# Two logarithms moved from ScalarE's table to a series on VectorE, in a two-block transformer kernel, with the four phases' issue orders rewritten

## The reference

```python
def rg_lru_group(xa, ya, conv_w, conv_b, ga_w, ga_b, gx_w, gx_b, lam):
    ...
    log_a = -LRU_C * r.astype(jnp.float32) * jax.nn.softplus(-lam.astype(jnp.float32))
    a = jnp.exp(log_a)
    ...

def forgetting_attention_group(q, k, v, f_logit, f_bias):
    ...
    log_f = jax.nn.log_sigmoid((f_logit + f_bias).astype(jnp.float32))
    ...
    c = jnp.cumsum(log_f, axis=1).transpose(0, 2, 1)
```

## Time and profile before

| | us |
|---|---|
| median of 3 runs | 962.14 (959.21 to 962.55) |
| the profiled execution | 962.55 |
| its span, first to last instruction | 960.8 |
| mixer, to the end of the output product | 0 to 212 |
| feed-forward, then the two layers | to 400, 680 and the end |

### The profile page before, as it was taken

The page is one execution under the profiler, slowest core; times in us unless marked ns, Lnnn a source line. Parts: engine busy times, 40 slices in busy tenths (PEclk is TensorE's granted clock), DMA queues, the critical chain, the costliest instruction groups (busy, mean ns, idle before and its releaser), DMA issues.

```text
span 960.8 us, 19359 instructions
## 1 busy us (share of the span) xinstructions
PE 923.4 (96%) x7806; PEld 852.2 (89%) x7806; DVE 702.0 (73%) x1061; ACT 522.7 (54%) x939; POOL 223.3 (23%) x194
## 2 busy tenths in 40 slices
PE   6899998889999999989999999999899999999997
PEld 6887996688999998879999899999699998999995
DVE  5887985558898897477877775576658787655684
ACT  7555264445665665374655574545555665555443
POOL 2324522232122121003314040033023322310140
PEclk9899998898999999999999999999999999999999
DMA  8433220043555556537545426555374444545551
GB/s 313 141 123 111 67 78 16 1 155 132 177 195 178 183 172 192 186 114 300 169 160 176 152 80 208 180 194 181 117 285 156 153 154 134 174 154 189 185 176 44
DMA packets 41560, 150.18 MB, mean 156 GB/s; under 512 B 4608, under 2 KB 4864, under 8 KB 41216
## 3 DMA queue, kind: packets, MB, share of 16 engines
q1 hardware_dynamic: 39456, 141.54, 43.9%
q10 hardware_dynamic: 2016, 7.41, 2.1%
HBM read 147.88 MB, written 1.05 MB: 155 GB/s over the span
## 4 chain that ended last, share of the span: by engine, by line
PE 92%; DVE 4%; ACT 2%; issue 1%; DMA 0%; DVEq 0%; SPq 0%; ACTq 0%
PE ps L724 90%; PE ps L1019 2%; DVE wlo L1637 1%; PE ps L1122 0%; DMA raw<-in_ws 0%; ACT whi L1233 0%; DVE S L1637 0%; DVE rw_pe L1862 0%; ACT L1233 0%; DVE ht L1645 0%; DVE rw_X L1637 0%; DVE pcraw L1637 0%; ACT tmp L1233 0%; DVE rr L1679 0%; DVE AR L1637 0%
## 5 line engine op out<-in xcount | busy, mean ns | idle before, releaser
L1233 ACT ACTIVATE whi<-raw 128x1024 fp32r<-128x1024 f32 (+1 forms) x264 | 278.2, 1055 | 314.9 <-PE ps L724 308.4
L724 PE MATMUL ps<-xh,whi 128*128 128x256 f32 (+2 forms) x1408 | 406.9, 289 | 20.5 <-DVE wlo L1637 8.2
L1637 DVE TENSOR_TENSOR wlo<-raw,whi 128x1024 fp32r<-128x1024 f32 (+1 forms) x256 | 324.4, 1271 | 114.6 <-ACT whi L1233 113.8
L724 PE MATMUL ps<-xl,whi 128*128 128x256 f32 (+2 forms) x1408 | 401.6, 285 | 1.4 <-DVE xl L1645 1.3
L724 PE MATMUL ps<-xh,wlo 128*128 128x256 f32 (+2 forms) x1408 | 400.8, 285 | 0.0
L724 PEld LDWEIGHTS ps<-xh,whi 128*128 128x128 f32 x1408 | 268.9, 191 | 26.5 <-issue 20.6
L724 PEld LDWEIGHTS ps<-xl,whi 128*128 128x128 f32 x1408 | 268.3, 191 | 2.6 <-DVE xl L1645 2.0
L724 PEld LDWEIGHTS ps<-xh,wlo 128*128 128x128 f32 x1408 | 269.2, 191 | 0.0
L724 PE MATMUL ps<-yh,whi 128*128 128x256 f32 x232 | 65.3, 281 | 0.0
L2213 POOL TENSOR_TENSOR gts<-gts 128x256 f32<-128x256 f32 x32 | 30.3, 955 | 150.5 <-DVE gts L1645 149.9
L724 PE MATMUL ps<-yl,whi 128*128 128x256 f32 x232 | 65.2, 281 | 0.0
(11 more groups left out here) (337 smaller groups left out, 1320.9 us busy)
## 6 DMA issues: line engine op xcount, KB each, us to landing
raw<-in_ws SPq DMA_DIRECT2D x262, 512.0 KB, 3.5
h<-in_rel ACTq DMA_DIRECT2D x2, 1024.0 KB, 13.2
qc<-in_gam ACTq DMA_DIRECT2D x3, 512.0 KB, 5.1
mt<-in_m ACTq DMA_DIRECT2D x2, 576.0 KB, 5.9
h<-in_hT SPq DMA_DIRECT2D x4, 272.0 KB, 5.4
gts<-in_lng ACTq DMA_DIRECT2D x2, 512.0 KB, 7.6
out<-ht SPq DMA_DIRECT2D x4, 256.0 KB, 2.0
gts<-in_g ACTq DMA_DIRECT2D x2, 448.0 KB, 10.0
```

Source lines behind the costliest of these rows:

```text
L724: return e.matmul(o, l, r, start=start, stop=stop, skip_group_check=True)
L1233: return e.activation(o, a, f, bias=bias, scale=scale, accum_out=acc)
L1637: return e.tensor_tensor(o, a, b, op)
```

## The change

Three edits are made.

1. ACT's Ln goes, in `la_a` and in `fo_log`. ACT still takes Abs and Exp.
2. DVE computes log(1 + u) as 2 atanh(u / (u + 2)) in a new helper `log1p`, 13 operations in three parts of 4, 5 and 4, each operation waiting for the one before. It is run once on 128x2 (steps `la.a`, `la.b 0`, `la.b 1`) and once on 8x272 (steps `fo.log 0` to `fo.log 2`). The factor 2 is taken up by `fo.sum` and `la.c`.
3. The strings of `WEAVE` for the mixer and for both layers are new; those of the feed-forward are as before. The steps are the same but for those of edit 2.

```diff
-        "f": [("fo.proj",), ("fo.log",), ("fo.sum",), ("fo.lr",)],
+        "f": [("fo.proj",)] + [("fo.log", n) for n in range(3)] + [("fo.sum",), ("fo.lr",)],
...
-        "n": [("la.a",), ("la.c",)],
+        "n": [("la.a",), ("la.b", 0), ("la.b", 1), ("la.c",)],
...
         "dve": (
-            "dmwddwddwddwddsndwwwwddfdmmmdfdmwwdsdmwdwmmdwmdwdwwddrrrwrwrfwwrreeeoeeorsrrrworwdsswssrddrrrddloo"
+            "dmwnnnndddddwwwdsdddwdwwdddwfmmdmmfsddwwrrrwdddrrrdfwrdwwddwrsffrwwrrwmmrmfrwwmssederrwssssreeeosss"
...
-            def fo_log():
-                sc.wait_ge(("fo.x",))
-                act(la[1], la[0], ACT.Abs).then_inc(*sc.says(("fo.abs",)))
-                sc.wait_ge(("fo.abs",))
-                act(la[1], la[1], ACT.Exp, scale=-1.0).then_inc(*sc.says(("fo.e",)))
-                sc.wait_ge(("fo.e",), ("c.ones",))
-                act(la[2], la[1], ACT.Ln, bias=ones[0:8, 0:1]).then_inc(*sc.says(("fo.l",)))
+            def fo_log(n):
+                if n == 0:
+                    sc.wait_ge(("fo.x",))
+                    act(la[1], la[0], ACT.Abs).then_inc(*sc.says(("fo.abs",)))
+                    sc.wait_ge(("fo.abs",))
+                    act(la[1], la[1], ACT.Exp, scale=-1.0).then_inc(*sc.says(("fo.e",)))
...
-                sc.wait_ge(("lr.e",), ("c.ones",))
-                act(lam4[:, 1, :], lam4[:, 0, :], ACT.Ln, bias=ones[:, 0:1]).then_inc(*sc.says(("lr.l",)))
...
+            def log1p(name, v, part, after):
+                u, s, z, q = v
+                n = [0, 4, 9][part]
+                d.wait_ge(after if part == 0 else (name, n - 1))
+
+                def then(t):
+                    t.then_inc(*d.says((name, n)))
+                    d.wait_ge((name, n))
+                    return n + 1
+
+                if part == 0:
+                    n = then(ts(s, u, 2.0, ADD))
+                    n = then(e.reciprocal(s, s))
+                    n = then(tt(s, s, u, MUL))
+                    n = then(tt(z, s, s, MUL))
+                else:
+                    if part == 1:
+                        n = then(ts(q, z, 1.0 / 17, MUL))
+                    for j in ((15, 13, 11, 9), (7, 5, 3))[part - 1]:
+                        n = then(stt(q, q, 1.0 / j, z, ADD, MUL))
+                    if part == 2:
+                        n = then(stt(s, q, 1.0, s, ADD, MUL))
...
+            def fo_log(n):
+                log1p("fo.l", la[1:5], n, ("fo.e",))
...
-                d.wait_ge(("fo.min",), ("fo.l",))
-                stt(x, s, -1.0, x, MUL, ADD).then_inc(*d.says(("fo.f",)))
+                d.wait_ge(("fo.min",), ("fo.l", 12))
+                stt(x, s, -2.0, x, MUL, ADD).then_inc(*d.says(("fo.f",)))
...
+            def rate(part):
+                log1p("lr.l", [lam4[:, i, :] for i in range(4)], part, ("lr.e",))
...
-                d.wait_ge(("lr.s1",), ("lr.l",))
-                stt(o, lam4[:, 1, :], 4.0, o, MUL, ADD).then_inc(*d.says(("lr.sp",)))
+                d.wait_ge(("lr.s1",), ("lr.l", 12))
+                stt(o, lam4[:, 1, :], 8.0, o, MUL, ADD).then_inc(*d.says(("lr.sp",)))
```

53 lines of the change are left out of this document (27 added, 26 removed).

## The result

| | before | changed |
|---|---|---|
| median, us | 961.41 (959.21 to 963.39, 6 runs) | 966.6 (965.36 to 967.53, 6 runs) |
| ratio, 95% interval | | 1.0052 (1.0035 to 1.0068) |
| the profiled execution, and its span | 962.55, 960.8 | 964.8, 963.1 |

The changed kernel is slower by 0.5%, some 5 us, and the interval of the ratio lies wholly above 1. A second measurement gave the same (1.0053). The forecast was a gain, to 960.3. Single executions of one kernel differ by 2 to 10 us, so two profiles can't be subtracted as they stand. The first profile of the changed kernel was faster than its six timed runs, that of before near its slowest, and they lie only 2.3 us apart. I therefore use both profiles of the changed kernel, called here "first" and "again" (the second).

A forecast was written before the change was run, and what follows sets the result against it. PE was taken as the bound, with only the mixer's waits and low clock able to move; +2.0 (start and first copy) +1.0 (middle) -5.3 (scan) = -2.3 from 962.55 gave 960.3 us, range 954.5 to 968.

The forecast's parts named there:

- Start: Mixer's start: work on `lam` ahead of the first `xl` makes PE's second matmul later by 3.5 us, bounds +2.5 to +4.5.
- first copy: First copy of a tile: less work ahead of it gives back 1.5 us; PE restarts at 30.5, after a 2.1 us wait.
- Middle: Mixer's middle: new DVE operations delay copies PE waits for, net +1.0 us, bounds -1.1 and +4.
- The wait I feared: Mixer's middle, near 56 us: PE waits 1.0 us for the seventh tile's copy, behind `rw.unit` on DVE.
- The second: Mixer's middle: a like wait at the three banks of the value tiles, put at 1.0 us.
- Scan: Scan, 151 to 175 us and `rw.o`: idle PE -1.0, low clock -3.3, block 4's transposition -1.0, together -5.3 us.
- the sign named for a miss: Prediction is wrong if PE waits over 3 us in the middle or the scan still has two low-clock stretches.
- rival 4: Scan: the new order does not fill it, idle and clock stay as before (+1.0 +3.3), 964.6 us; chance 0.15.
- The third term: Scan: block 4's transposition, 1.04 us, moves behind the second `rw.o`, where PE waits anyway; -1.0 us.
- The mixer's end: From the end of `rw.o` to the output product, some 12 us from 175 to 186.66: stays as it was.
- Layers: The two layers, where PE never waits: 0 us, with 0 to +3 that can be lost.
- Rival 1: Mixer's middle: POOL holds up the series on DVE, PE's bank waits grow up to 6 us, low clock follows; 968, chance 0.14.

The follow-up runs named there:

- the kernel with `late 1` moved: The kernel before, with POOL's `late 1` placed behind both `rw.fin` steps instead of between them; 962.01 us, ratio 1.0026.
- the first try of the series in the old order: The changed kernel's code with the kernel before's queue orders, `fo.log 1` behind `cols`, the steps on `lam` around `xya 0` and `xya 1`; 965.87 us, ratio 1.0051.

## Why the prediction failed, step by step

**Start, +3.5, and first copy, -1.5: the sum came out, with the start mis-sized and some luck.** DVE's first operation on `lam` started at 8.40, as worked out. The sixteen took 4.1 us and not 3.05 (3.12, from 18.36 to 21.48, in the kernel that has them where `la.c` stood). The eight in the middle, and the one that met POOL's 11.37:

```profile
9.40 2.07 DVE L1642 SCALAR_TENSOR_TENSOR lam<-lam 128x2 f32<-128x2 f32 x8
11.50 0.66 DVE L1639 TENSOR_SCALAR lam<-col 128x2 f32<-128x2 f32 x1
```

```profile
11.37 0.76 POOL L2241 TENSOR_TENSOR tmp<-tmp 128x272 f32<-128x272 f32 x1 [0.70 <-ACT tmp L1233]
```

So the second matmul started at 13.0 and not at 12.0, at the upper bound of +4.5. The table load took its 1.28 us (from 6.87), and the next activation started at 8.16, 0.01 behind it: the trace stays against the 1380 ns of drain that the Trainium skill (ScalarE: Activation LUTs, What ACT_TABLE_LOAD costs) states. The restart came at 30.39 (30.92 again) for 30.5, behind a wait of 2.03 us:

```profile
30.39 0.40 PE L724 MATMUL ps<-xh,whi 128*128 128x272 f32 x1 [2.03 <-DVE pcraw L1634]
```

That the extra 1 us of the start did not reach the restart is luck: the matmuls' pace doubled 3.1 us after the second matmul in the first profile and 4.3 in the second, 4.5 before (last section). The prediction calls that first pace "low clock"; the clock column reads 1.00 there. And +2.0 holds against one profile of the kernel before: against the restart at 27.49 of the kernel with `late 1` moved it would be +2.9.

**Middle, +1.0: near in size, wrong in place.** The wait I feared, for the seventh tile's copy at 56, was 0.14 us, at 53.4. The second, which I only put at 1.0 by likeness, was the real one: 1.65 and 1.51 us for `kT`. (My own terms, 1.0 + 1.0 - 1.1, make 0.9.) I had found the queue position and not POOL's two steps beside it, and I had argued DVE's room from 99.52 of 122.00 us, an average that says nothing of the 24 us from 36 on, where 5.4 us were left before and 0.4 now. Without the series that wait was 0.49 to 0.57 us in three kernels, so the series' own part in it is about 1 us. What I had left out is the clock behind such a wait, 0.91 over 20 us in the second profile, 1.8 us.

**Scan, -5.3: wrong, the main error.** The step "it is better placed: ... I count idle PE of 1.7 us" failed: it was 3.15 us. The order put more fill into the chain, but on DVE `late 0` and `at f 4 0` stood ahead of the chain's own operations, and PE waited 1.33 us at `rw.scanU 3`:

```profile
162.53 0.49 PE L724 MATMUL ps<-rw_X,rw_kk 64*64 64x64 f32 x8 [1.33 <-DVE rw_X L1634]
```

I had followed PE's queue there and not DVE's. The step "I expect one stretch of 3.4 us at 1.2 GHz" failed too: from 150 to 180 us the clock mean was 0.83 in the kernel before and in both profiles of the changed one. There were 10.2 us at 1.2 GHz each time, in two stretches (3.4 and 6.8 us) before and in one of 10.2 in both profiles of the changed kernel. So the sign named for a miss, two low stretches, did not come, nor did 3 us of waits in the middle, and the term failed all the same. The number of stretches is not the order's either: with the orders of before and `late 1` moved it was one, of 10.2. I had priced the clock as if it followed from the idle time, by 3.3 us, on no row that shows it; with the wait at `rw.scanU 3` at 0.56 the mean was still 0.83. That was rival 4, to which I gave 0.15; with its 4.3 us the sum is 964.6. The third term, -1.0 for the transposition, is not what failed: from the first `rw.o` to `rw.mean 0` PE took 7.08 us before (from 168.51) and 5.63 now (from 170.42), again 6.17.

**The mixer's end, "this part stays": wrong, +2.0.** I looked at DVE's `xl` and its place behind the second division, which did not change. PE's row there in the earlier trace rows names the releaser that came last, DVE's, out at 186.30; the same tile has a half on POOL, which had been out 1.1 us earlier. POOL's row before:

```profile
184.43 0.77 POOL L2213 TENSOR_TENSOR xl<-qT,xh 128x272 fp32r<-128x272 f32 x1
```

The new order on POOL put it behind `rw.fin 1`, so that it came out at 189.06, 2.2 us behind DVE's half (186.81), and no step of mine looked at POOL's queue there. Two runs, one in each direction, show it: 1.5 to 1.6 us at the place.

**Layers, 0: right.** PE's longest sums of waits behind 245 us are 1.5 and 1.4 us in the first profile, 1.6 and 1.5 in the second (1.6 before), and taking the layers' orders back changed nothing.

**Sum.** Forecast -2.3. With the two failed steps at what they measured (scan about 0, end +2.0) it reads +2.0 +1.0 +0 +2.0 = +5.0, against 5.2 between the medians. That it fits to 0.2 us is luck. The common window of middle and scan changed by -1.4 us in the first profile and by +2.0 in the second, and in the old order it was 147.07 once and 144.75 in the kernel with `late 1` moved, with as much idle PE (3.75 and 4.01 us), so by the clock. What stands firm is the loss itself, the 1.5 us at the mixer's end, and that start and end put back together bring the kernel level. Rival 1 (the series meets POOL) is real as a mechanism: in the first try of the series in the old order four operations of `fo.log 1` took 4.02 us, 1.82 in the changed kernel. In the changed kernel two products of `fo.log 0` took 3.13 us beside a `wlo` of POOL, and PE did not wait behind them; the series' cost there is its length at the start and its part in the wait for `kT`. The rival's "a wait of over 2 us brings low clock with it" does not hold in these runs (last section).

## What to carry to other kernels

When a change rewrites issue orders, walk through every engine's queue at the few places where the main engine waits, also that of the engine that is busy a quarter of the time: the releaser that a row names is only the last of several, and the next order may make another one last. Read an engine's room in the 20 us where the work goes, not over 120. Book no gain of clock unless a row shows what brings it. And when two steps on DVE are short and dependent, ask first what POOL runs beside them: put such a chain where POOL rests, or give its time as POOL's.
